# Column-form norms with POOL Newton roots, a one-pass softmax combination, and reordered mixing projections in a two-layer hybrid trunk

## What is computed

```python
u = h @ w_in                                     # q, k, v, conv (a, gate), fourier
s = einsum('bhiqd,bhikd->bhiqk', qb, k) * HEAD_DIM ** -0.5      # i: two maps
p = softmax(s);  p_diff = p[:, :, 0] - lam * p[:, :, 1]
o = einsum('bhqk,bhkd->bhqd', p_diff, v)
a = rmsnorm(o, g_subln) * (1.0 - lam_init)       # over the 128 of one head
y = a_conv * sigmoid(gate);  y = depthwise_conv(y, width 31) + b_dw
y = silu(layernorm(y) * g_ln + b_ln) @ w_pw + b_pw              # over 256 channels
f = real(fft2(u_f)) @ w_f + b_f
x = x + mx[5] * concat([a, y, f]) @ w_out
```

## Time and profile before

| | us |
|---|---|
| median of 3 runs | 2882.47 |
| lowest and highest | 2881.99, 2888.78 |
| the profiled execution | 2883.3 |
| its span, first to last instruction | 2881.4 |

### The profile page before, as it was taken

How to read it: one execution, slowest core, us unless ns; L and a number is a source line. 1 busy time by engine, 2 the same in 40 slices (tenths; PEclk the granted TensorE clock), 3 DMA queues, 4 the chain that set the end, 5 groups by cost and what they waited for, 6 DMA issues and landing times.

```text
span 2881.4 us, 37801 instructions
## 1 busy us (share of the span) xinstructions
PE 2730.6 (95%) x15288; PEld 2307.6 (80%) x15288; DVE 1731.1 (60%) x2338; ACT 784.4 (27%) x1078; POOL 177.6 (6%) x136
## 2 busy tenths in 40 slices
PE   6999999999986999999999999999999977899998
PEld 4888888879844778888888788888888845888887
DVE  5655656574967475655656756565445866544445
ACT  4212111132156431112112411111224156322222
POOL 1000000030010210000000200000011011200001
PEclk7999999999999999999999999999999989999999
DMA  7532333312001123332322223333121101133221
GB/s 265 177 116 87 112 107 102 103 45 74 30 30 59 45 70 121 102 102 90 129 88 88 83 93 106 112 101 102 44 88 59 45 30 59 59 104 101 87 88 44
DMA packets 180753, 255.32 MB, mean 89 GB/s; under 512 B 5310, under 2 KB 128812, under 8 KB 180652
## 3 DMA queue, kind: packets, MB, share of 16 engines
q1 hardware_dynamic: 180652, 253.90, 27.3%
HBM read 251.78 MB, written 2.10 MB: 88 GB/s over the span
## 4 chain that ended last, share of the span: by engine, by line
PE 87%; DVE 6%; ACT 3%; POOL 2%; issue 1%; SPq 1%; DMA 0%; ACTq 0%; DVEq 0%; POOLq 0%
PE ps L860 27%; PE ps L861 27%; PE ps L862 27%; PE ps L1125 1%; POOL sqsum L851 1%; PE ps L1205 1%; PE ps L1233 1%; DVE e L2017 1%; DVE nb L2027 1%; DVE h_lo L1681 1%; ACT e L1542 1%; PE ps L1001 1%; ACT w_hi L1311 1%; PE ps L1219 1%; PE ps L1174 1%
## 5 line engine op out<-in xcount | busy, mean ns | idle before, releaser
L860 PE MATMUL ps<-h_hi,w_hi 128*128 128x512 f32 (+1 forms) x3040 | 1044.6, 344 | 10.9 <-DVE h_lo L1681 9.3
L861 PE MATMUL ps<-h_lo,w_hi 128*128 128x512 f32 (+1 forms) x3040 | 1041.3, 343 | 0.0
L862 PE MATMUL ps<-h_hi,w_lo 128*128 128x512 f32 (+1 forms) x3040 | 1039.8, 342 | 0.0
L860 PEld LDWEIGHTS ps<-h_hi,w_hi 128*128 128x128 f32 x3040 | 579.7, 191 | 81.5 <-issue 9.7
L861 PEld LDWEIGHTS ps<-h_lo,w_hi 128*128 128x128 f32 x3040 | 579.7, 191 | 66.0 <-issue 1.0
L862 PEld LDWEIGHTS ps<-h_hi,w_lo 128*128 128x128 f32 x3040 | 579.2, 191 | 66.0
L1780 DVE TENSOR_TENSOR prod<-sil,ps 128x512 f32<-128x512 f32 (+1 forms) x156 | 88.0, 568 | 638.4 <-PE ps L862 630.5
L860 PE MATMUL ps<-hid_hi,w_hi 128*128 128x512 f32 (+1 forms) x1248 | 432.9, 347 | 0.0
L861 PE MATMUL ps<-hid_lo,w_hi 128*128 128x512 f32 (+1 forms) x1248 | 429.2, 344 | 0.0
L862 PE MATMUL ps<-hid_hi,w_lo 128*128 128x512 f32 (+1 forms) x1248 | 429.0, 344 | 0.0
L1311 ACT ACTIVATE w_hi<-raw 128x2048 fp32r<-128x2048 f32 x158 | 297.0, 1906 | 474.5 <-PE ps L862 474.5
(11 more groups left out here) (138 smaller groups left out, 1959.2 us busy)
## 6 DMA issues: line engine op xcount, KB each, us to landing
side_raw<-in_w_ada SPq DMA_DIRECT2D x120, 512.0 KB, 3.7
raw<-in_w_ffn_gate SPq DMA_DIRECT2D x44, 1024.0 KB, 5.3
raw<-in_w_ffn_up SPq DMA_DIRECT2D x44, 1024.0 KB, 5.3
raw<-in_w_ffn_down SPq DMA_DIRECT2D x44, 1024.0 KB, 4.9
raw<-in_w_in SPq DMA_DIRECT2D x14, 1024.0 KB, 5.3
ada_buf<-in_w_ada SPq DMA_DIRECT2D x9, 1024.0 KB, 10.5
raw<-in_w_out SPq DMA_DIRECT2D x8, 1024.0 KB, 6.7
raw<-in_w_in SPq DMA_DIRECT2D x8, 512.0 KB, 4.7
```

The lines of the kernel that those rows point to most:

```text
L860: mm(out, wh, xh, start=start, stop=False)
L861: mm(out, wh, xl, start=False, stop=False)
L862: return mm(out, wl, xh, start=False, stop=stop)
```

## The change

- **Projections.** PE's order in the mixer is K, conv, Q, V, Fourier input. K starts with the context columns of all four heads, then the latent columns of heads 0 and 1, then of 2 and 3 (`keys_first`). ACT copies all keys to `kT`, and DVE rotates from there. POOL splits the first two K tiles, as it did the first two V tiles.
- **Taps.** DVE rotates K first. The taps stand between the splits and the rotations of Q: 12 of channel group 0 alone, then 19 pairs, then 12 of group 1 alone.
- **Conv norm.** Mean, variance, scale and pointwise product move from the attention loop into `fourier`. The variance is made as a column: `csq` is the weight operand and one column of ones moves, 12 products of one column (8 in layer 1). POOL makes 1/sqrt of the column by a seed from the bits and three Newton steps, 13 instructions, and scales the identity by it, once for each 128 tokens (`diag`). A product of ones with `diag` spreads the scale over the channels.
- **One-pass combination.** DVE makes one column, minus lambda times the quotient of the two sums, and one pass `e0 = e1 * c + e0`. The first map stays undivided; the head norm takes that factor out, with the epsilon scaled by the square of its sum.
- **Head norm.** The products with the values give query rows, not query columns. DVE copies 128x128 to `onorm`, ACT squares it with a running sum, POOL makes the root in 12 instructions of one column and scales `onorm` in a thirteenth, each behind a wait for the one before. PE turns the result back (`turn_o`) in bank 6 six steps after the unit's scores, ACT and DVE make the high and low part. The last three units are turned in the output projection, ahead of head 3.
- **Splits.** The low parts of three output weight tiles move from POOL to DVE, into steps 5, 8 and 11.

```diff
-            def attention_help(l):
-                split(("out", l, 0))
-                split(("out", l, 1))
...
+            def conv_scales(l):
+                nt = sum(n for _, n in mix_segs(l)) // 128
+                x, y, t = cvar[:, 0:nt], nt_y[:, 0:nt], nt_t[:, 0:nt]
+                wait_freed(pool, ("var", l))
+                step(ts(y.bitcast(I32), x.bitcast(I32), -0.5, SEED, ALU.mult, ALU.add))
+                for _ in range(3):
+                    settle()
+                    step(ptt(t, y, y, ALU.mult))
+                    settle()
+                    step(ptt(t, t, x, ALU.mult))
+                    settle()
+                    step(ts(t, t, -0.5, 1.5, ALU.mult, ALU.add))
+                    settle()
+                    step(ptt(y, y, t, ALU.mult))
+                settle()
+                for i in range(nt):
+                    ts(diag[:, i, :], ident[:], nt_y[:, i:i + 1], None, ALU.mult).then_inc(diag_ready, 1)
+            def head_scale(l, u):
+                i = u % 8
+                x, y, t = nt_x[:, i:i + 1], nt_y[:, i:i + 1], nt_t[:, i:i + 1]
+                s0 = esum[:, i, 0:1]
+                pool.wait_ge(osq_done, units_before(l) + u + 1)
+                step(ts(t, s0, s0, EPS, ALU.mult, ALU.mult))
+                settle()
+                step(ts(x, osq[:, i:i + 1], 1.0 / 128, t, ALU.mult, ALU.add))
+                settle()
+                step(ts(y.bitcast(I32), x.bitcast(I32), -0.5, SEED, ALU.mult, ALU.add))
+                for n in range(3):
+                    settle()
+                    step(ts(t, y, y, x, ALU.mult, ALU.mult))
+                    settle()
+                    step(ts(t, t, -0.5, 1.5, ALU.mult, ALU.add))
+                    settle()
+                    if n < 2:
+                        step(ts(y, y, t, None, ALU.mult))
+                    else:
+                        step(ts(oscale[:, i:i + 1], y, t, None, ALU.mult))
+                settle()
+                ts(onorm[:, u % 4, :], onorm[:, u % 4, :], oscale[:, i:i + 1], None, ALU.mult).then_inc(o_scaled, 1)
...
+            def turn_o(l, u):
+                wait_bank(pe, ("OT", l, u))
+                pe.wait_ge(o_scaled, units_before(l) + u + 1)
+                nc.tensor.transpose(ps[:, 6, 0:128], onorm[:, u % 4, :], ident[:]).then_inc(products, 1)
...
+                                if k == HEADS - 1 and s == 0:
+                                    for u in late_units(l):
+                                        turn_o(l, u)
...
-                    step(dve_.reciprocal(rs[:, p, :], sums[:, p, :]))
+                    step(dve_.reciprocal(rs[:, i % 2, 1:2], esum[:, i % 8, 1:2]))
                     settle()
-                    step(dve_.tensor_scalar(e1[:, p, 0:n], e1[:, p, 0:n], rs[:, p, 1:2], neglam[:, l:l + 1], ALU.mult, ALU.mult))
+                    step(dve_.tensor_scalar(c, rs[:, i % 2, 1:2], esum[:, i % 8, 0:1], neglam[:, l:l + 1], ALU.mult, ALU.mult))
                     settle()
-                    stt(out=e0[:, i % 3, 0:n], in0=e0[:, i % 3, 0:n], scalar=rs[:, p, 0:1], in1=e1[:, p, 0:n],
+                    stt(out=e0[:, i % 3, 0:n], in0=e1[:, i % 2, 0:n], scalar=c, in1=e0[:, i % 3, 0:n],
                         op0=ALU.mult, op1=ALU.add).then_inc(p_ready, 1)
...
+                for i in range(len(us) + OT_LAG):
+                    if 0 <= i - OT_LAG < len(us):
+                        head_low(i - OT_LAG)
+                    if i < len(us):
+                        maximum(i)
+                    if 1 <= i <= len(us):
+                        combine(i - 1)
+                    if 0 <= i - O_LAG < len(us):
+                        take_o(i - O_LAG)
+                    if i in (5, 8, 11):
+                        split(("out", l, (5, 8, 11).index(i)))
```

More of the change, by code:

```diff
@@ L1107, in fourier, with conv_mean @@
                 ms = mix_segs(l)
+                ns = len(ms)
+                nt = sum(n for _, n in ms) // 128
+                before = 2 * segs_before(l)
                 small = raw_of(("W", l))[:].rearrange("p (i k n) -> p i k n", i=4, k=2)
+                def conv_mean():
+                    pe.wait_ge(acc_ready, 2 * (l + 1))
+                    for s, (o, n) in enumerate(ms):
+                        ao = 0 if s == 0 else C_CTX - HALF
+                        wait_bank(pe, ("mean", l, s))
+                        for c in range(2):
+                            last = mm(pt(("mean", l, s), n), ones[:], acc[:, c, ao:ao + n], start=(c == 0), stop=(c == 1))
+                        last.then_inc(products, 1)
@@ new lines, in point_wise @@
+                def point_wise():
+                    for p in range(2):
+                        for s, (o, n) in enumerate(ms):
+                            ao = 0 if s == 0 else C_CTX - HALF
+                            wait_bank(pe, ("pw", l, p, s))
+                            pe.wait_ge(cs_done, before + 2 * s + 2)
+                            for c in range(2):
+                                last = mm(pt(("pw", l, p, s), n), small[:, 0, c, 128 * p:128 * p + 128], acc[:, c, ao:ao + n],
+                                          start=(c == 0), stop=(c == 1))
+                            last.then_inc(products, 1)
@@ L1179, in attention @@
                 ms = mix_segs(l)
[L1180 to L1181 removed]
+                u_before = units_before(l)
+                e_before = 2 * u_before
                 slots = score_slots(l)
@@ L1423, in copy, with sigmoids @@
                     act_fn(dst, pt(key, n), ACT.Copy, scale=scale).then_inc(bank_free[bank_of(key)], 1)
[L1425 to L1434 removed]
+                nt = sum(n for _, n in ms) // 128
+                def sigmoids(c):
                     for s, (o, n) in enumerate(ms):
@@ L1559, in mix @@
-                    beside(i)
-                    if i in (3, 4, 14):
-                        split(next(rest))
-                hbefore = HEADS * sum(len(mix_segs(x)) for x in range(l))
-                for h in range(HEADS):
-                    for s, (o, n) in enumerate(ms):
-                        act.wait_ge(ht_done, hbefore + h * ns + s + 1)
-                        act_fn(h_hi[:, h, o:o + n], qT[:, h, o:o + n], ACT.Copy).then_inc(mix_hi_done, 1)
-                split(next(rest))
+                    if i in (4, 7, 10):
+                        split(("out", l, (4, 7, 10).index(i)))
@@ new lines, in mix @@
+                split(("Q", l, 1))
+                for i in range(4, 12):
+                    tap(0, i)
+                glu(1)
+                both_taps(0, 4)
+                split(("V", l, 0))
+                both_taps(4, 8)
+                rotate_q(0)
+                rotate_q(1)
+                split(("V", l, 1))
+                both_taps(8, 14)
+                rotate_q(2)
+                rotate_q(3)
+                split(("four", l))
+                both_taps(14, 19)
+                for i in range(19, TAPS):
+                    tap(1, i)
@@ L2043, in mix @@
                 q = 3 * l + 2
-                for _ in range(3):
-                    next(rest)
                 first, second = seg_order(q)
@@ L2058, in mix @@
                     if (v, s) == (0, ns - 1):
-                        split(next(rest))
+                        split(("out", l, 3))
                     if (v, s) == (1, ns - 1):
```

665 lines of the change are left out of this document (338 added, 327 removed).

## The result

The changed kernel takes 2896.27 us (median of five runs, 2895.29 to 2900.58), the kernel before 2882.36 beside it: a ratio of 1.0048, 95% interval 1.0033 to 1.0063. It is slower by half a per cent, where 2863.5 and faster was forecast. The profiled execution has a span of 2894.2 us, against 2881.4.

A forecast was written before the change was run, and what follows sets the result against it. POOL's head-norm chain was taken to bound both attentions: 2883.3 less 4.3 in layer 0 and 14.7 in layer 1 gives 2864.3, as a median 2863.5 us. The range was 2832 to 2908.

The forecast's parts named there:

- the price of a POOL instruction: Head norm in the attention: each dependent one-column POOL instruction was taken at 0.29 us.
- POOL's chain as the bound: Attention of both layers: POOL busy 119.5 and 84.9 us, ending later than the ring's marks 943.0 and 2423.7.
- the unit's price: POOL's head norm for one unit: 13 x 0.29, 0.11 for 127 more columns, 0.14 for ACT's signal, 4.0 us.
- Both bounds: Price of a POOL column instruction: 0.24 us from below (fill plus gap), 0.33 from above (additions with two wide inputs).
- the rivals: The one meant, POOL is dearer: scalar columns make an instruction 0.37, a unit 5.06, the sum 2906 us; slower, chance 0.23.
- DVE in the way: Attention: DVE's combination delays POOL 0.89 us a latent unit, 0.35 a context unit; the three splits 6.5.
- `fourier`: Stage ahead of the attention, now with the conv norm: first score 14.2 us later in layer 0, 8.7 in layer 1.
- The taps' cover: Layer 0: last tap at some 770 us, PE needs it at 786, so 16 us of cover.
- The gain of K ahead of V: Projections: second latent root asked for a little sooner, 0.9 us for each layer, from 0 to 3.
- The ring without POOL: Attention: 4.5 us a latent, some 2.4 a context unit; 112.9 and 91.6 us from first score to head 3.
- POOL is hidden: Rival: an instruction costs 0.24 us or less, the ring's pace sets both marks, 2829 us; chance 0.25.
- 40 P - 179.2: The change in us for a POOL unit's price P: 3.4 gives -44, 4.5 gives +2, the break at 4.48.

The follow-up runs named there:

- forms experiment: Changed kernel with the same 13 POOL instructions for each unit, four in another form (three products and a square as tensor_tensor): 2880.79 us, ratio 0.9997.
- the kernel with one iteration: Changed kernel with one Newton iteration for each head scale instead of three, the root left inexact: 2849.45 us, ratio 0.9885.
- the kernel with ACT's tail order: Changed kernel with ACT's square of a unit ahead of an older unit's high part, behind the last scores only: 2892.51 us, ratio 1.0034.

## Why the prediction was wrong

**The step that failed is the price of a POOL instruction.** The mechanism, POOL's chain as the bound, was right; the term of the sum that was mis-sized is the unit's price. The prediction took 0.29 us, half-way between a fill and an addition of two wide inputs, and a unit of 4.0. Both bounds lacked the operand that these instructions have, a column as scalar. Measured from start to start: 0.28 to 0.30 with immediates or with two tensor columns, 0.37 to 0.38 with one scalar column, 0.42 to 0.43 with two; the mean over a round is 0.37, the unit 5.04. The twelve narrow instructions take 4.33 us, not 3.48, and the scaling of `onorm` 0.71 to the next start, not the 0.40 of the forecast; the 0.14 for ACT's signal doesn't show between units. That is 1.04 us a unit, 25 us in layer 0 and 16.6 in layer 1. The text named the cause of the larger part, among the rivals, and gave the time: 0.37, a unit of 5.06, 2906. The unit measured 5.04; the time was 10 us too high. The forms experiment shows that the operand is what costs: the same products with two tensor columns are 0.1 us shorter.

**DVE in the way** was priced 0.89 a latent unit. POOL's stretches (842.00 to 982.27 and 2360.84 to 2458.08, less the pauses) hold 5.73 and 5.94 us a unit, so blocking costs 0.7 and 0.9 with the splits in it: 16.6 and 14.4 us where 23.5 and 20.7 were forecast. A pass holds POOL only from the point where its next instruction starts: 0.34 and 0.13 us into the pass in the rows above, so 0.54 and 0.75 were lost there, not 0.89. The prediction's reading that a pass counts in full didn't hold.

**The pause ahead of the last unit**, 2.9 and 2.25 us, was not foreseen. Together: 25.0 - 6.9 + 2.9 = 21.0 against a miss of 19.9 in layer 0, and 16.6 - 6.3 + 2.25 = 12.6 against 14.8 in layer 1.

**The two ends of POOL's work** account for the rest, within 0.3 us in each layer. Its first unit begins 16.5 us behind the first score in layer 0 and 18.6 in layer 1, where 17.1 was forecast, and head 3 comes 0.25 and 1.4 us behind its last instruction, not 0.5. That is 0.8 less and 2.4 more. No term of the forecast stood for the clock, and the later start in layer 1 goes with it: in layer 0 the clock was granted in full, while in layer 1 two stretches of the first steps read (length, PE, PEld, DVE, ACT, POOL busy, granted clock, DMA share, GB/s)

```profile
2346.00:2350.00 4.00, 2.11 (x8) 0.70 (x8) 1.85 (x3) 1.57 (x4) 0.00 (x0) 0.58 0.00 0
2350.00:2354.00 4.00, 3.59 (x11) 1.67 (x11) 2.16 (x4) 1.20 (x5) 0.00 (x0) 0.57 0.00 0
```

At 0.57 the scores at 2350.19 take 2.93 us, not 1.56. Why the clock fell stays open: PE had idled 2.08 us ahead of the scores at 2345.89, but it had idled as long at the same place in layer 0 (2.07 us, ahead of 829.12), and there it didn't fall.

**`fourier`** was 3.2 and 1.8 us cheaper: the variance 2.73 us for 24 narrow products, 0.114 each, where the nearest row gave 0.175; the pointwise products 5.3, not 6.2. The root of the conv norm took 7.25 us, not 5.6: its 13 narrow instructions have immediates or two tensors and cost 0.29 each, as priced, but each of the six scalings of the identity took 0.59, where some 0.3 was taken. It still ended 0.9 us before the spread. The taps' cover held: DVE had waited 19.9 us for the mean's products when they came.

**The gain of K ahead of V** can't be told. Layer 1 shows none (1329.0 us on both sides). Layer 0's start is 2.3 us earlier, but kernels that are alike up to there differ by 3 (Z from 785.2 to 788.1).

**The ring without POOL**: the step was right, 4.55 for 4.5, but the splits were 6.5 us a layer on DVE alone, where ACT's part costs a step too, 8.5. From first score to head 3 it needs 122 and 102 us, not 113 and 92. So the rival "POOL is hidden" would have given about 2849, the time of the kernel with one iteration, and not 2829.

**What was right**: POOL as the bound in both layers, PE's idle time ahead of the turn, no table loads between the exponentials (one is left in each layer, six before in layer 0), the 1.0 us pass that holds POOL, and the shape of the sum: 40 P - 179.2 gives +22.4 at P = 5.04; less 13.2 for the blocking and 5.0 for `fourier`, with 5.1 for the pauses, +9.3; the two ends of POOL's work add 1.6. The span grew by 12.8; the other 1.9 are spread over the remaining stages. The last of them is 2.6 longer, but before's mark there is itself an estimate. The fault was to take the middle of two bounds neither of which contained the operand in question.

## What to carry to other kernels

Before a serial chain of small instructions is moved to an idle engine, count it times the units and compare it with the step it must fit in: here 13 instructions against a step of 4.5 us, so that by the forecast's own sum 0.05 us an instruction decided the sign. Price the exact form, scalar operands too, and let an unlike form only move the range to one side. Then shorten the chain before anything else; and cut a long side job into pieces that fit the slack of each step, on every engine that has a part in it.

## What the runs showed of the hardware

- POOL, one column of 128 partitions: 0.19 us with immediates, 0.19 as tensor_tensor, 0.27 to 0.29 with one column as scalar, 0.34 with two, each with some 0.1 us of gap behind it in a dependent chain (behind the scaling of 128 columns the next one starts 0.71 us later with a column as scalar, and 0.56 us later as tensor_tensor). Six columns cost as much as one (0.20, conv's root). 128 columns with a scalar column: 0.62.
- A DVE pass with one SBUF input at 0.62 us for 768 elements holds POOL off like one with two inputs. Against a whole weight split an instruction of 0.19 us took 2.20:

```profile
846.56 2.20 POOL L884 TENSOR_SCALAR nt_t<-nt_t 128x1 f32<-128x1 f32 x1
```

 An instruction that POOL starts up to 0.09 us ahead of DVE's is held all the same:

```profile
886.22 2.44 POOL L882 TENSOR_SCALAR nt_t<-nt_y,nt_x 128x1 f32<-128x1 f32 x1
...
886.31 2.30 DVE L1748 TENSOR_TENSOR w_lo<-raw,w_hi 128x2048 fp32r<-128x2048 f32 x1
```

- PE's clock fell behind the wait of 4.71 us. Two stretches behind the last turn of layer 0 in the changed kernel (length, PE, PEld, DVE, ACT, POOL busy, granted clock, DMA share, GB/s):

```profile
982.00:986.00 4.00, 3.58 (x11) 3.03 (x12) 1.64 (x3) 0.37 (x1) 0.27 (x1) 0.50 0.47 126
986.00:990.00 4.00, 4.00 (x28) 4.00 (x27) 0.22 (x1) 0.00 (x0) 0.00 (x0) 0.73 0.35 136
```

 and the first such stretch of the kernel with ACT's tail order, whose last wait is 2.03:

```profile
977.00:981.00 4.00, 3.46 (x24) 3.23 (x25) 1.73 (x3) 0.37 (x1) 0.40 (x1) 1.00 0.48 130
```

 At 0.50 (1.2 GHz) a product takes 0.63 us. Yet from head 3 to the first score of layer 1 both need the same, 1359.7 and 1359.4 us, so this dip of the clock cost nothing in the end. That the lost time was covered by what PE waits for later on is likely, but not shown.
